# Turning the order of two matrix products in every second chunk of a split-precision linear layer

## What the kernel computes

```
def swiglu(h, w1, w3, w2):
    return (jax.nn.silu(h @ w1) * (h @ w3)) @ w2        # 1024 -> 2816 -> 1024
```

## Time and profile before

| what | value |
|---|---|
| median of three runs | 3000.43 us |
| time of the profiled execution | 3012.29 us |
| span of the profiled execution | 3010.5 us |
| TensorE matmul busy | 2866.8 us, 95% of the span, 22916 instructions |
| TensorE weight load busy | 2543.4 us, 84% |
| VectorE busy | 2081.5 us, 69% |
| ScalarE busy | 1455.2 us, 48% |
| mean DMA rate | 173 GB/s |
| mean granted TensorE clock | 0.968 of full speed |

### The profile page before, as it was taken

How to read it: one execution, slowest core, us unless ns; L and a number is a source line. 1 busy time by engine, 2 the same in 40 slices (tenths; PEclk the granted TensorE clock), 3 DMA queues, 4 the chain that set the end, 5 groups by cost and what they waited for, 6 DMA issues and landing times.

```text
span 3010.5 us, 53944 instructions
## 1 busy us (share of the span) xinstructions
PE 2866.8 (95%) x22916; PEld 2543.4 (84%) x22916; DVE 2081.5 (69%) x3259; ACT 1455.2 (48%) x1957; POOL 148.2 (5%) x257
## 2 busy tenths in 40 slices
PE   5999999989999999999899999999999999999998
PEld 5888899978888888998788877889788888887887
DVE  5986757758878767576686577764676668658774
ACT  2545644545445455445454355544554345435552
POOL 1000000100000000002000022000100000004000
PEclk7999999999999999999999999999999999999999
DMA  8875326537768753265375443655265546562453
GB/s 257 259 245 165 114 76 211 180 117 239 241 201 261 240 159 109 93 207 179 113 225 184 153 157 102 194 181 174 94 195 182 169 155 208 182 200 71 154 179 101
DMA packets 516703, 521.43 MB, mean 173 GB/s; under 512 B 16503, under 2 KB 513728, under 8 KB 516464
## 3 DMA queue, kind: packets, MB, share of 16 engines
q1 hardware_dynamic: 513856, 517.28, 53.7%
q0 software_dynamic: 816, 0.27, 0.1%
q10 hardware_dynamic: 1792, 0.44, 0.1%
HBM read 516.90 MB, written 1.05 MB: 172 GB/s over the span
## 4 chain that ended last, share of the span: by engine, by line
PE 83%; DVE 9%; ACT 5%; issue 2%; DMA 1%; POOL 0%; ACTq 0%; SPq 0%; DVEq 0%; POOLq 0%
PE P L65 81%; DVE wsp L74 4%; ACT wsp L71 2%; PE P L68 1%; ACT arena L71 1%; DVE ACC L82 1%; DVE arena L82 1%; DVE arena L74 1%; DVE X L74 1%; DMA raw<-in_nsa_w_in 1%; ACT L71 0%; ACT HX L71 0%; DVE HX L82 0%; DVE X L82 0%; DMA raw<-in_ada_w 0%
## 5 line engine op out<-in xcount | busy, mean ns | idle before, releaser
L65 PE MATMUL P<-HX,wsp 128*128 128x512 f32 (+1 forms) x10304 | 1632.1, 321 | 39.2 <-DVE wsp L74 12.9
L65 PEld LDWEIGHTS P<-HX,wsp 128*128 128x128 f32 x10304 | 1466.3, 194 | 183.7 <-issue 22.2
L74 DVE TENSOR_TENSOR wsp<-raw,wsp 128x2048 fp32r<-128x2048 f32 (+4 forms) x440 | 946.2, 2152 | 380.1 <-ACT wsp L71 379.6
L71 ACT ACTIVATE wsp<-raw 128x2048 fp32r<-128x2048 f32 (+4 forms) x440 | 790.6, 1799 | 557.2 <-PE P L65 502.4
L65 PE MATMUL P<-FG,wsp 128*128 128x512 f32 (+1 forms) x2816 | 502.0, 340 | 1.4 <-DVE wsp L74 1.4
L65 PEld LDWEIGHTS P<-FG,wsp 128*128 128x128 f32 x2816 | 430.7, 188 | 67.7 <-DVE wsp L74 2.6
L71 ACT ACTIVATE arena<-P 128x512 f32<-128x512 f32 (+3 forms) x384 | 214.4, 568 | 552.7 <-PE P L65 551.7
L74 DVE TENSOR_TENSOR arena<-arena,P 128x512 f32<-128x512 f32 (+2 forms) x232 | 151.1, 653 | 197.4 <-ACT arena L71 164.0
L65 PE MATMUL P<-arena 64*64 64x64 f32 (+9 forms) x4000 | 242.3, 264 | 17.8 <-ACT arena L71 10.0
L65 PEld LDWEIGHTS P<-arena 64*64 64x64 f32 (+3 forms) x4000 | 192.3, 148 | 65.2 <-issue 31.9
L82 DVE SCALAR_TENSOR_TENSOR ACC<-raw,sm,ACC 128x256 f32<-128x256 f32 x476 | 230.8, 485 | 16.7
(11 more groups left out here) (110 smaller groups left out, 1373.4 us busy)
## 6 DMA issues: line engine op xcount, KB each, us to landing
raw<-in_ffn_w SPq DMA_DIRECT2D x120, 1024.0 KB, 5.3
raw<-in_ada_w SPq DMA_DIRECT2D x72, 1024.0 KB, 5.0
raw<-in_w_in SPq DMA_DIRECT2D x52, 1024.0 KB, 5.2
raw<-in_ffn_w_gate SPq DMA_DIRECT2D x44, 1024.0 KB, 5.2
raw<-in_ffn_w_up SPq DMA_DIRECT2D x44, 1024.0 KB, 5.2
raw<-in_ffn_w_down SPq DMA_DIRECT2D x32, 1024.0 KB, 5.0
raw<-in_nsa_w_in SPq DMA_DIRECT2D x20, 1024.0 KB, 7.0
raw<-in_ffn_w SPq DMA_DIRECT2D x16, 768.0 KB, 4.4
```

What stands on the lines that cost most here:

```text
L65: return self if self.e is None else self.e.matmul(*a, skip_group_check=True, **k)
L71: return self if self.e is None else self.e.activation(*a, **k)
L74: return self if self.e is None else self.e.tensor_tensor(*a)
```

## The change

In every chunk with an odd number, the narrow product of the low weights is issued ahead of the wide one of the high weights. In chunks with even numbers, the order stays. The call in `lins` is not touched. The number, the size and the operands of the matmuls are the same as before. The first chunk of a tile, which starts the sum in the bank, is never turned.

```
-        def two(e, o, wh, wl, x, xh, first, last):
+        def two(e, o, wh, wl, x, xh, first, last, turned=False):
+            if turned:
+                e.matmul(o[:, 0:xh.shape[-1]], wl, xh, start=False, stop=False)
+                return e.matmul(v3(o, 2), wh, x, start=False, stop=last)
             e.matmul(v3(o, 2), wh, x, start=first, stop=False)
             return e.matmul(o[:, 0:xh.shape[-1]], wl, xh, start=False, stop=last)
...
-                    ins = two(e, tile_of(p, m), wh[:, kk, s], wl[:, kk, s], X2[:, :, kk, :], X2[:, 0, kk, :], kk == 0, kk == k - 1)
+                    ins = two(e, tile_of(p, m), wh[:, kk, s], wl[:, kk, s], X2[:, :, kk, :], X2[:, 0, kk, :], kk == 0, kk == k - 1, kk % 2)
...
-                                ins = two(e, tile_of(p, mm), wh[:, kk, w], wl[:, kk, w], FG[:, :, c, :], FG[:, 0, c, :], c == 0, c == 21)
+                                ins = two(e, tile_of(p, mm), wh[:, kk, w], wl[:, kk, w], FG[:, :, c, :], FG[:, 0, c, :], c == 0, c == 21, c % 2)
```

## The result

The changed kernel took 2986.01 us (median of six runs, 2984.53 to 2994.42); the kernel before took 3005.73 us (median of six, 3000.39 to 3014.19). The recorded ratio is 0.9944, with a 95% interval of 0.9931 to 0.9956: 0.56% faster. (The two medians by themselves stand at 0.9934; in the larger sets of the experiments the kernel before has medians of 3002.56 and 3002.64 us.) The forecast was 3001 us, no measurable change.

The account below looks back on a forecast made before the run. TensorE's gapless order of matmuls was taken as the bound. From the profiled 3012.3 us, 2176 turned cycles at 693.3 to 706.7 ns gave 2986.4 to 3015.4 us; the middle, 700 ns, gave 3001 us, range 2984 to 3020.

Parts of the forecast that it names:

- no change: Whole kernel: any time within about 0.5%, 2985.4 to 3015.4 us, can't be told from no change; chance 0.64.
- The sum made in the profiled execution's time: Whole kernel: from the profiled 3012.3 us, 3015.4 all slow, 2986.4 all cycles quick, middle 3000.9 us.
- The price of a cycle: Two turned chunks on TensorE: 693.3 to 706.7 ns, as before; middle 700 ns, over 2176 cycles.
- narrow behind narrow: Step between two narrow matmuls in a turned cycle: 120.0 ns, taken from a stretch of narrow matmuls only.
- Half of the cycles at either rate: Turned stretches: the new order meets the same two rates, half of its cycles at each, giving 3001 us.
- About 0.5% is what a measurement of this kernel can tell: Whole kernel: 15 us either way, 2985.4 to 3015.4 us, counts as no change.
- What bounds the kernel: TensorE, busy for 95% of the span and 83% of the chain; a nanosecond per pair counts in full.
- The two rates of the old order: Wide and narrow pairs in feed-forward stretches: 353.3 or 346.7 ns a pair, held for a hundred microseconds and more.
- Own price: Turned cycles: each matmul keeps its price whatever follows, one load beside each step; 2986.4 to 3015.4 us, chance 0.64.
- The ends of tiles and the wait for split weights: Tile ends: sums 10 ns later, 0.1 us in all; third matrix: the wait gives back a sixth of a gain.
- The faster rival: Turned cycles: wide to wide is cheap, 220 ns or less, cycle 686.7 ns or less, 2971.9 us; chance 0.16.
- The slower one: Turned cycles: two narrow steps leave loads behind, 713.3 ns, 3029.9 us, or always the slower rate; chance 0.20.

Follow-up runs that it names:

- units alone: Against the changed kernel, only the weight units of lin_wide stay turned and the third matrices get the old order back; ratio 0.9967, 2992.5 us.
- one and two chunks in four: In place of every odd chunk, only chunk 1, or chunks 1 and 2, of each four are turned; ratios 1.0019 and 0.9978.

## Why the prediction was wrong

The time, 2986.01 us, lies inside the range of 2984 to 3020 us, and the cycle, 696.8 ns, inside the 693 to 707 that the prediction set as its own sign. What failed is "no change". Three steps led to it.

- **The sum made in the profiled execution's time was given as the median: wrong, and the larger error.** The sum goes from 3012.3 us down to 3000.9, a gain of 11.4 us or 0.38%. The prediction then set 3001 us beside the median of 3000.4, and the gain was gone. It saw the 11.9 us between the two, ascribed them to the two rates, as not shown, and put the same offset of the changed kernel at nothing. The changed kernel's profiled execution too lies above its median, by 8.4 us (2994.42 against 2986.01). The first three times of before also flattered the forecast: the six of the comparison have a median of 3005.73 us, against which 3001 is 0.2% less.
- **The price of a cycle was mis-sized, 700 ns where 696.8 were measured: 3.2 ns x 2176 = 7.0 us.** The term behind it is narrow behind narrow, taken as 120.0 ns from a stretch of narrow matmuls only the earlier trace rows and measured as 114.6 amid wide ones. The others were nearly right: wide behind wide 232.9 ns, where 226.7 to 233.3 had been taken, and the old pair of steps 349.2 ns, where the middle was 350. "Half of the cycles at either rate" failed as well: the new order doesn't meet the two rates but has one of its own, in all stretches shown.
- **"About 0.5% is what a measurement of this kernel can tell": wrong.** The recorded ratio has an interval of about 0.13% to either side, and gains of 0.33% (units alone) were told from none.

3001 us less 7.0 and less 8.4 is 2985.6 us, 0.4 from the result. The two terms are measured after the fact, so this shows that they suffice, and not that they could have been foretold.

- **What bounds the kernel: right.** TensorE's order is on the path, and 19.2 us less of its busy time went with 17.9 us less of span.
- **The two rates of the old order: right.** They were read properly as 353.3 and 346.7 ns a pair. Some pairs of the first feed-forward part ran quick as well (groups of 64 at 69, 81 and 118 us with 11.34 to 11.37 us, where 11.58 is usual), about 0.6 us that the sum leaves out.
- **Own price: wrong as a mechanism, though off by only a few ns.** "Each matmul keeps its own price whatever follows it" doesn't hold: a narrow step measured 114.6 to 120.0 ns and a wide one 231.8 to 236.5 in the orders with full loads whose steps are listed, the same neighbours gave 706.6 and 700 ns (one and two chunks in four), and a shorter load reversed the sign of the turn. That each step has one load beside it in either order is true and doesn't fix the price.
- **The ends of tiles and the wait for split weights.** The wait in the third matrix is 0.35 us, between the 0.24 and 0.39 of the earlier trace rows, as foretold. Over the whole kernel such waits grew by 1.4 us. The 10 ns at tile ends can't be seen.
- **The faster rival** asked for a cycle of 686.7 ns or less and isn't what happened. **The slower one**, two narrow steps in a row leaving loads behind, was wrong for full loads: the new order stayed below 706.7 ns, and the step behind two narrow ones wasn't late (115.9 ns from narrow to wide).

The Trainium skill says in "TensorE: Matmul & The Clock Gate", section "Back-to-back issue gap", that in a stream of loads and matmuls the spacing is set by both. The traces agree: with shorter loads the old order's pair was seen at 340, 346.7 and 350 ns, and no longer at 353.3. The same page's section "Step-by-step: what each phase is for" says that loading the next weights doesn't steal read bandwidth from the running matmul, since TensorE has two read ports. The runs can't show the ports; they show that the length of a load changes the price of the stream.

**What stays open** is the mechanism inside TensorE: why a stream of identical pairs has two steady rates, what puts it into one, and why the slower was seen only with both loads at full length. For full loads, the runs exclude the columns in PSUM, the layout of the activations, the place in the program, the number of changeovers and the pairs of neighbours as sole causes. Whether the other engines' traffic or the moment at which a stretch starts picks the rate wasn't tried.

## What to carry to other kernels

Where one engine is busy without a gap, the same instructions can still run at more than one steady rate, so compare several equal stretches of a trace, and a second trace, before a price is taken from one of them. The order of matmuls of unlike length is worth a trial of each candidate: here orders of the same 4608 pairs cost 693.3 to 706.7 ns for two chunks, and no rule about neighbours foretold which. Read a price in several parts of the trace: the last stretches of the kernels with shorter loads hid rates that their earlier ones had. And take the price of a step from the same surroundings as far as there are any; 120.0 ns from a stretch of like matmuls became 114.6 amid unlike ones. Last, a forecast made from a profiled execution is a difference: it is to be set against that execution's own time, or the offset to the median goes into it, taken from several runs.

## What the runs showed of the hardware

- One stream of alternating 512 and 256 column matmuls, each with a load of 128 columns, ran at 353.3 or at 346.7 ns a pair at full clock, for a hundred microseconds and more, and in another execution of the same program the same stretch had the other rate. With one of the two loads at 64 or 16 columns it ran at 340, 346.7 or 350 ns, and nowhere at 353.3.
- The turned order had one rate in all stretches shown, 696.8 ns for two chunks. With a shorter load it cost 687 to 707 ns, and more than the old order in the same stretch each time (by 6.6 to 13 ns).
- A narrow matmul behind a narrow one took 120.0 ns in a stretch of narrow ones, and 114.6 ns in the turned order, with operands of the same size.
- Where the narrow product is summed in the bank, and whether a wide matmul reads 512 elements in one piece or two, made no difference (113.30 and 113.31 us against 113.31).
